# Hybrid decoder layer on one core: gate thirds placed in front of seven of the last state-space group's eight samples, five taken from the other groups

## What is computed

```python
proj = x @ w_in                         # c_q, c_kv, k_pe, z, xbc, dt_raw, g_logits
# state-space branch: 4 groups of 8 heads; prompt in chunks, then per sample:
#   y   += C . old_state * exp(a_cum)           (8 samples of 4 tokens)
#   new  = old_state * exp(a_sum) + B^T . (x dt decay)
yg    = rms_norm((y + xs * d_skip) * silu(z))   # z: 16 tiles of 128 features
gates = sigmoid(g_logits + b_gate)              # g_logits: 16 tiles of 128 features
merged = g_a * (attn @ w_branch_a) + g_b * (yg @ w_branch_b)
```

## Time and profile before

| what | value |
|---|---|
| median of 3 runs | 3004.88 us (2998.44 to 3005.58) |
| profiled execution, device time | 2995.18 us |
| its span | 2993.3 us |
| PE busy | 2855.1 us (95%) |
| granted PE clock, mean | 0.968 |

### The profile page before, as it was taken

The page is one execution under the profiler, slowest core; times in us unless marked ns, Lnnn a source line. Parts: engine busy times, 40 slices in busy tenths (PEclk is TensorE's granted clock), DMA queues, the critical chain, the costliest instruction groups (busy, mean ns, idle before and its releaser), DMA issues.

```text
span 2993.3 us, 45619 instructions
## 1 busy us (share of the span) xinstructions
PE 2855.1 (95%) x18828; PEld 2562.1 (86%) x18828; DVE 1532.1 (51%) x2076; ACT 771.4 (26%) x1197; POOL 1024.6 (34%) x587
## 2 busy tenths in 40 slices
PE   8899999999999998999999989999899999999996
PEld 7789999899989995555666689999799999999996
DVE  2774887664746554555344357865652222222227
ACT  1211221353535443555332222110220000000004
POOL 3543333332323322444211123444233333333330
PEclk9999999999999997999899989999899999999997
DMA  4154223574755535222334243353111111111101
GB/s 139 46 158 148 79 86 110 160 188 132 185 144 166 148 114 152 64 63 74 138 127 189 93 146 136 109 180 111 54 36 50 43 47 46 43 50 43 44 28 58
DMA packets 314166, 308.87 MB, mean 103 GB/s; under 512 B 31813, under 2 KB 272714, under 8 KB 311498
## 3 DMA queue, kind: packets, MB, share of 16 engines
q1 hardware_dynamic: 252008, 194.57, 22.9%
q10 hardware_dynamic: 58394, 73.89, 7.2%
q0 software_dynamic: 3584, 37.75, 3.3%
HBM read 227.96 MB, written 78.20 MB: 102 GB/s over the span
## 4 chain that ended last, share of the span: by engine, by line
PE 67%; DVE 12%; issue 10%; POOL 5%; ACT 4%; DMA 1%; SPq 0%; ACTq 0%; POOLq 0%; DVEq 0%
PE ps L908 41%; PE ps L1068 10%; POOL pr L854 4%; DVE cv L2199 3%; PE ps L1348 2%; PE ps L1324 2%; PE ps L1304 2%; DVE cv L2193 1%; PE ps L1147 1%; PE ps L1101 1%; DVE cv L2201 1%; PE ps L1105 1%; PE ps L979 1%; PE ps L1094 1%; ACT so L1696 1%
## 5 line engine op out<-in xcount | busy, mean ns | idle before, releaser
L751 POOL TENSOR_TENSOR whi<-raw,cst 128x1024 fp32r<-128x1024 f32 x160 | 312.0, 1950 | 1162.9 <-PE ps L908 959.9
L753 POOL TENSOR_TENSOR wlo<-raw,whi 128x1024 fp32r<-128x1024 f32 x160 | 431.2, 2695 | 12.6
L908 PE MATMUL ps<-ahi,whi 128*128 128x352 f32 x1728 | 376.4, 326 | 5.7 <-issue 3.5
L908 PE MATMUL ps<-alo,whi 128*128 128x352 f32 x1728 | 375.7, 326 | 0.0
L908 PE MATMUL ps<-ahi,wlo 128*128 128x352 f32 x1728 | 372.8, 324 | 0.0
L908 PEld LDWEIGHTS ps<-ahi,whi 128*128 128x128 f32 x1728 | 294.9, 190 | 7.4 <-issue 4.7
L908 PEld LDWEIGHTS ps<-ahi,wlo 128*128 128x128 f32 x1728 | 297.0, 190 | 0.0
L908 PEld LDWEIGHTS ps<-alo,whi 128*128 128x128 f32 x1728 | 295.5, 188 | 0.0
L1068 PE MATMUL ps<-xhi,whi 128*128 128x352 f32 x768 | 257.0, 335 | 0.6 <-ACT xraw L1693 0.4
L1068 PE MATMUL ps<-xhi,wlo 128*128 128x352 f32 x768 | 248.7, 324 | 0.0
L1068 PE MATMUL ps<-xlo,whi 128*128 128x352 f32 x768 | 248.6, 324 | 0.0
(11 more groups left out here) (363 smaller groups left out, 5143.8 us busy)
## 6 DMA issues: line engine op xcount, KB each, us to landing
raw<-in_w_in SPq DMA_DIRECT2D x61, 512.0 KB, 5.1
s_a<-d_acum SPq DMA_DIRECT2D x32, 512.0 KB, 7.1
d_xbc<-so ACTq DMA_DIRECT2D x24, 528.0 KB, 2.7
gt<-d_g SPq DMA_DIRECT2D x24, 528.0 KB, 3.7
raw<-in_w_ffn_gate SPq DMA_DIRECT2D x22, 512.0 KB, 3.8
raw<-in_w_ffn_up SPq DMA_DIRECT2D x22, 512.0 KB, 3.8
raw<-in_w_ffn_down SPq DMA_DIRECT2D x22, 512.0 KB, 3.6
d_z<-zo ACTq DMA_DIRECT2D x16, 528.0 KB, 4.9
```

Source lines behind the costliest of these rows:

```text
L751: pool.tensor_tensor(whi[s][:, :], raw[:, u], ones[:, 0:1].broadcast_to([P, UNIT]), ALU.mult).then_inc(sem("unit_hi"), k["unit_hi"].adds(1))
L753: pool.tensor_tensor(wlo[s][:, :], raw[:, u], whi[s][:, :].bitcast(F32), ALU.subtract).then_inc(sem("unit_split"), k["unit_split"].adds(1))
L908: last = pe.matmul(ps[0:m, 3 * b + c, 0:width], w(j), x[:, j, at:at + width], start=i == 0, stop=i == n - 1)
```

## The change

Which samples have a third in front of them is set by `third_with`, and by it alone:

```diff
     def third_with(g, q):
 
-        return g < SG - 1 or q < 8 - LEAD
+        return q not in (3, 6)[0:2 - g % 2] if g < SG - 1 else q < 7
```

## The result

| what | before | changed kernel |
|---|---|---|
| median, same session | 3003.09 us (20 runs) | 3012.97 us (3009.05 to 3023.79, 20 runs) |
| profiled execution, its span | 2995.18, 2993.3 | 3014.46, 3012.7 |

The account below looks back on a forecast made before the run. PE, busy 95% of the span, and its clock were taken to bound the kernel. The terms -20.2 + 19.4 + 1.8 + 10.0 gave +11.0 us on the median 3004.88, forecasting 3016 us, range 3001 to 3024.

Parts of the forecast that it names:

- Five thirds out: Groups 0 to 2: five thirds of 4.03 us each leave PE's path, -20.2 us.
- Waits that the thirds covered: Groups 0 to 2: PE's waits at samples 3 and 6 show without their thirds, +1.8 us (0 to 2.9).
- The clock, five falls of 2.0 each: Groups 0 to 2: PE's clock falls at each of the five thinned places, +10.0 us (0 to 16.5).
- The first rival: Groups 0 to 2: the clock holds, as PE stays busy; +2.1 us in all, no visible change; chance 0.14.
- What moves besides: DVE, POOL's splits, SP's weight loads and ACT's outputs: shifts of order or position that cost nothing.
- The end of group 3: SP's attention loads wait for the later last third, so the exponentials start later, +19.4 us (+11.9 to +20.8).
- The credit of 1.4 us for fewer stores: End of group 3: 1.4 us taken off the +20.8 because the DMA engines have less to do.
- Rival 2: Start of the attention: the loads do not hold it, the engines decide at +11.9; +3.5 us in all; chance 0.13.
- Rival 4: Groups 0 to 2: the clock falls early at all five places for the double stretch; +17.8 us in all; chance 0.06.
- Rival 5: Group 3: it keeps falling to half clock despite its thirds; no size or chance given.
- rival 3: Clock holds, loads do not hold the attention, and its first scores start at full clock; -9.1 us in all; chance 0.04.

Follow-up runs that it names:

- x2: The changed kernel, with SP issuing the attention's second head pair's loads after ssm_over instead of before it; 1.0006 of the kernel before.
- x3: The kernel before, with the same five thirds taken out of groups 0 to 2 but put ahead of group 0, group 3 untouched; 1.0028 of before.
- x6: The changed kernel, with SP issuing chunk 2's loads of groups 1 to 3 ahead of the sample step's loads and a weight load; 1.0013 of before.
- x8: The kernel before with chunk 2's loads early, second head pair's loads after ssm_over, and three thirds (ahead of sample 3, groups 0 to 2) moved to group 3; 0.9969 of before.
- x11: The changed kernel, with any weight load in chunk 1 of groups 1 to 3 issued behind chunk 3's loads; 1.0027 of the kernel before.
- x4: The changed kernel, with eight dense matmuls of unused result added ahead of each of the five thinned samples; 1.0059 of the kernel before.
- x5: The kernel before, with SP issuing chunk 2's loads of groups 1 to 3 ahead of the sample step's loads and a weight load; 0.9976 of before.
- x10: The kernel before, with the weight load at group starts issued right behind chunk 2's loads instead of ahead of chunk loads; 0.9999 of before.
- x9: The kernel before, with five thirds moved into group 3 from the six ahead of group 0, groups 0 to 2 keeping theirs; 1.0057 of before.
- x1: The kernel before, with SP issuing the attention's second head pair's loads after ssm_over instead of before it; 0.9987 of before.

## Why the prediction held, point by point

The number came out, and so did the two large terms, the thirds out of groups 0 to 2 and the end of group 3. That the rest met it as closely in this profile is in part luck.

**Five thirds out, -20.2 us.** Right in size: a thinned sample that waits for nothing takes 2.23 us, one with its third 6.28.

**Waits that the thirds covered, +1.8.** Right: 0.16 three times and 0.89 twice in groups 0 to 2, 2.3 us (L1147 on L2340). The forecast worked with 0.24 and 1.1, the first of them misread: the row itself has 0.15, as the transposes end 0.66 us after their start and not 0.58.

**The clock, five falls of 2.0 each, +10.0.** Right as a mechanism, wrong in number and size for this profile. The clock of 0.50 behind sample 3, forecast for each of the three groups, came in one: two of five thinned places fell, one for 6.8 us (9.45 - 6.49 = 3.0 us lost), one for 3.4 (1.7 lost): 4.7 us. Over the six profiles that have a thinned sample 3 in groups 0 to 2 (the change, x2, x3, x6, x8, x11) the clock fell there at 11 of 18, at a cost of 1.5 to 3.1 us, 2.6 on average. Behind the sample 7 that follows a thinned sample 6 (the same without x8) it fell at 8 of 10, each time for 3.4 us, worth 1.7. The five profiles with all five places lost 4.7, 7.9, 12.5, 6.2 and 8.0 us there, 7.9 on average. So the forecast's 10.0 was near the mean, though not as five falls of 2.0: three or four of five places fell, for 1.5 to 3.1 each. The first rival (the clock holds) is wrong: x3 gave back 16.4 of its 20.2 us. Of the rule of the Trainium skill ("TensorE: Matmul & The Clock Gate", Part 1) it was said there that, read as busy time, it leaves the clock at full speed in these samples. The trace after speaks against that reading once more, 3.30 us busy of 3.30 just ahead of the fall at group 2's sample 3, and x4 against the idea that the gaps do it.

**What moves besides, nothing.** This step failed. PE waited 5.3 us for s_a instead of 3.0, and two falls followed (worth 3.4 us of full speed). That is 5.7 us in this profile. At group 1's start a weight load stands behind chunk 2's loads and explains a part; at group 2's none does. The term filled what the clock term had too much, so the sum for groups 0 to 2, -20.2 + 2.3 + 4.7 + 2.3 + 3.4 = -7.5, met both the measured -7.4 and the forecast -8.4: two errors of about 5 us cancelled, which is luck. In x2 and x11, with the same order of thirds, it came out otherwise: four of five places fell, 7.9 and 8.0 us, the loads cost 1.0 and 0.8 more than before (shorter waits, one fall), and groups 0 to 2 won 8.8 and 9.4. So over several executions the loads count for less than in this profile, as x6 against x5 and x10 suggest too.

**The end of group 3, +19.4.** Right: +20.5 in the profile (+19.9 in x9, +20.4 in x6 against x5; x4 and x11 have 60.1 and 63.9 where the change has 62.2), with SP released 20.9 later (forecast 20.8) and y's store issued 12.1 later (11.9). What the forecast did not say is that y's store now goes out in the midst of the loads and so takes 17.2 us to land. The credit of 1.4 us for fewer stores is not to be told from nothing.

**Rival 2** (the engines decide, not the loads) is excluded by x1 and x2, and by PE's wait of 11.7 us for the first pair's loads, for this order of loads. **Rival 4** (five long falls) is what x3 came close to; in the changed kernel it was one. **Rival 5** didn't come about: group 3's samples ran 6.27 us each at clock 1.00. Nor did **rival 3**: the clock was at 0.50 from 1146.1 on, and the first scores, after that wait, ran at it.

## What to carry to other kernels

Dense work in front of sparse work hides more than that work's waits: here it also kept the clock up for what lies around it, so taking it out of one place cost part of its time again there (16.4 of 20.2 us in x3). Such falls should be priced as a chance times a cost, and the chance read from several profiles. A last piece of dense work that gates a load should not be put at the end of a stage without a look at that load: here all of its delay, 20.9 us, reached the next stage. And where units of work are moved against a loop, look at which bulk load now stands right behind which urgent one on the loading queue; issuing the urgent load as soon as its buffer is free gave 0.24% by itself (x5).

## What the runs showed of the hardware

- The granted clock fell to 0.50 behind work in which PE was busy all the time (3.30 us of 3.30 ahead of 978.8 in the changed kernel: matmuls with 4 moving columns, transposes, and matmuls with 32 rows), and stayed there through the dense third behind (6.51 of 6.60 us busy). At such places it fell in some executions and groups and not in others (at sample 3 in 11 of 18, behind sample 7 in 8 of 10). In the state-space stage these falls lasted 3.4 or 6.8 us.
- A single wait of PE of about 2 us in otherwise dense work may be followed by a fall of some 3.4 us. After 2.08 and 2.44 us in the changed kernel, 1.97 in x2, 2.92 in x3, 2.06 and 3.09 in x4, 1.86 in x9 and 2.06 in x11 it was; after 1.63 in the kernel before, 1.94 in x1, 1.75 in x4, 1.78 and 3.16 in x9, and 1.52 and 2.11 in x10 it was not. At group 2's start it fell in three kernels with the changed kernel's pattern (the change, x2, x11; not in x4, which has the filler) and in none with that of before (before, x1, x10), at waits of about the same length, so the length alone doesn't decide. What does is open.
- A 64 KB store landed in 2.3 us (x1), 8.8 (before), 9.9 (x2) or 17.2 us (the change), by how many large loads on the other queue it ran beside.
